# RWKV-7 group of a hybrid decoder: the token mean taken from the turned values, the state's products accumulated in PSUM, the square taken by ScalarE

## The reference, cut to what matters

```
def step(S, inp):                      # for each of the 512 tokens
    r_t, w_t, k_t, v_t, kk_t, a_t = inp
    sa = einsum('bhvk,bhk->bhv', S, -kk_t)
    S = S * w_t[:, :, None, :] + sa[..., None] * (kk_t * a_t)[:, :, None, :] + v_t[..., None] * k_t[:, :, None, :]
    return S, einsum('bhvk,bhk->bhv', S, r_t)
...
y = _wkv7_scan(r, decay, k, v, kk, a)
y = _group_norm(y, ln_w, ln_b, RW_GN_EPS) + sum(r * k * r_k, -1) * v
```

## Time and profile before

| | |
|---|---|
| device time, median of 3 runs | 2413.65 us (2412.28 to 2413.82) |
| the profiled execution's own time | 2416.05 us |
| its span, first to last instruction | 2414.3 us |
| granted TensorE clock, mean over the span | 0.99 |
| TensorE busy (matmul) | 2324.0 us, 96% of the span |
| GpSimd busy | 1737.8 us, 72% |
| VectorE busy | 1192.2 us, 49% |
| ScalarE busy | 634.9 us, 26% |

### The profile page before, as it was taken

The page is one execution under the profiler, slowest core; times in us unless marked ns, Lnnn a source line. Parts: engine busy times, 40 slices in busy tenths (PEclk is TensorE's granted clock), DMA queues, the critical chain, the costliest instruction groups (busy, mean ns, idle before and its releaser), DMA issues. The chain is left out here.

```text
span 2414.3 us, 38594 instructions
## 1 busy us (share of the span) xinstructions
PE 2324.0 (96%) x16160; PEld 1751.9 (73%) x16160; DVE 1192.2 (49%) x1515; ACT 634.9 (26%) x1133; POOL 1737.8 (72%) x1228
## 2 busy tenths in 40 slices
PE   7999999999999999899999999999999999989999
PEld 6767777777777777677777677777776777767777
DVE  5123346647464773565250323557375546735552
ACT  5222222212221222333341323222222212214421
POOL 3677688768577787687637666878586687877785
PEclk9999999999999999999999999999999999999999
DMA  4623253223234346432445233533242243473323
GB/s 156 187 80 104 83 161 110 84 81 114 84 89 132 118 131 233 151 92 71 148 112 160 79 114 92 154 93 102 66 121 82 81 150 108 131 275 110 86 77 125
DMA packets 164335, 285.09 MB, mean 118 GB/s; under 512 B 28664, under 2 KB 36216, under 8 KB 162624
## 3 DMA queue, kind: packets, MB, share of 16 engines
q1 hardware_dynamic: 108352, 180.93, 27.0%
q10 hardware_dynamic: 55808, 101.69, 12.4%
HBM read 230.89 MB, written 51.64 MB: 117 GB/s over the span
## 5 line engine op out<-in xcount | busy, mean ns | idle before, releaser
L733 POOL TENSOR_SCALAR w_hi<-raw 128x512 fp32r<-128x512 f32 x552 | 905.4, 1640 | 476.3 <-PE ps_proj L774 401.6
L743 POOL TENSOR_TENSOR w_lo<-raw,w_hi 128x512 fp32r<-128x512 f32 (+1 forms) x640 | 836.8, 1308 | 152.6 <-ACT w_hi L1237 97.1
L774 PE MATMUL ps_proj<-h_hi,w_hi 128*128 128x512 f32 (+1 forms) x1760 | 740.1, 421 | 2.0 <-POOL w_lo L743 0.9
L774 PE MATMUL ps_proj<-h_lo,w_hi 128*128 128x512 f32 (+1 forms) x1760 | 691.8, 393 | 0.0
L774 PE MATMUL ps_proj<-h_hi,w_lo 128*128 128x512 f32 x1728 | 678.5, 393 | 0.0
L774 PEld LDWEIGHTS ps_proj<-h_hi,w_hi 128*128 128x128 f32 (+1 forms) x1760 | 331.3, 188 | 113.1 <-issue 29.7
L774 PEld LDWEIGHTS ps_proj<-h_lo,w_hi 128*128 128x128 f32 (+1 forms) x1760 | 331.3, 188 | 75.0
L774 PEld LDWEIGHTS ps_proj<-h_hi,w_lo 128*128 128x128 f32 x1728 | 327.8, 190 | 68.6 <-issue 11.4
L789 PE MATMUL ps_proj<-w_hi,h_hi 128*128 128x512 f32 x448 | 181.1, 404 | 0.4 <-POOL w_lo L743 0.4
L789 PE MATMUL ps_proj<-w_hi,h_lo 128*128 128x512 f32 x448 | 174.9, 390 | 0.0
L789 PE MATMUL ps_proj<-w_lo,h_hi 128*128 128x512 f32 x448 | 174.5, 390 | 0.0
(11 more groups left out here) (349 smaller groups left out, 3132.5 us busy)
## 6 DMA issues: line engine op xcount, KB each, us to landing
raw<-in_w_in_dram SPq DMA_DIRECT2D x480, 256.0 KB, 2.7
raw<-in_w_out_dram SPq DMA_DIRECT2D x128, 256.0 KB, 3.0
projected<-stage ACTq DMA_DIRECT2D x116, 256.0 KB, 2.8
arena<-projected ACTq DMA_DIRECT2D x90, 256.0 KB, 3.1
out_dram<-arena ACTq DMA_DIRECT2D x7, 1024.0 KB, 4.8
gated_hi<-arena ACTq DMA_DIRECT2D x24, 256.0 KB, 2.6
gated_lo<-arena ACTq DMA_DIRECT2D x24, 256.0 KB, 3.2
h_hi<-gated_hi SPq DMA_DIRECT2D x8, 768.0 KB, 13.7
```

The source lines that it names most:

```text
L733: nc.gpsimd.tensor_scalar(hi, src, 1.0, None, ALU.mult).then_inc(s_hi_split, 1)
L743: nc.gpsimd.tensor_tensor(lo, src, hi.bitcast(F32), ALU.subtract).then_inc(s_raw_split, 1)
L774: last = mm(ps_proj[rows, m, :], lhsT, rhs, start=(k == 0 and j == 0), stop=(k == KT - 1 and j == len(products) - 1))
```

## The change

The mean is no longer taken from the output but from the values, when they lie turned in PSUM: VectorE sums each token's 64 elements (`tensor_reduce` to a new `rw_vmean`) and writes `rw_vT = v - sum / 64`, in place of ScalarE's copy. TensorE's mean product and its waits go. The state's products are added onto the local output in banks 2 and 3, for the chunks 1 to 7 alone (the state ahead of chunk 0 is zero), so VectorE's copy of the local output, its zero state and its two additions go. ScalarE squares the output in PSUM, VectorE multiplies it there by one over the root. The local products are issued in another order: all of the first kind, then those of the output, in which only the first tile's products carry `start`. Of the fills, `rw_v` goes from 2 to 4 tiles, `rw_carried` from 2 to 3, and `rw_mean` (3 tiles) goes.

```diff
-    rw_turned=(3, 3, 3, 3), rw_v=(2, 2, 2, 2),
+    rw_turned=(3, 3, 3, 3), rw_v=(4, 4, 4, 4),
-    rw_carried=(2, 2, 2, 2), rw_mean=(3, 3, 3, 3), rw_gate=(13, 14, 13, 12),
+    rw_carried=(3, 3, 3, 3), rw_gate=(13, 14, 13, 12),
+        y_parts = ps[:, 2:4, 256:512].rearrange("p c (i t) -> p c i t", i=NT)
...  TensorE
                         fill("rw_v", hp)
+                        pe.wait_ge(s_rw_turned_copied, 3 * hp + 3)
                         pe.wait_ge(s_rw_v_copied, hp + 1)
...
                             for c, q, h, half in quarters:
                                 mm(ps[half, 2 + c, own], rw_pu[...], rw_gb[...], start=True, stop=True)
+                        for i in range(NT):
+                            fed = slice(256 + i * 64, 256 + (i + 1) * 64)
                             for c, q, h, half in quarters:
-                                mm(ps[half, 2 + c, fed], rw_vT[...], rw_gk[...], start=True, stop=False)
+                                mm(ps[half, 2 + c, fed], rw_vT[...], rw_gk[...], start=(i == 0), stop=False)
                             for c, q, h, half in quarters:
-                                mm(ps[half, 2 + c, fed], rw_pu[...], rw_gb[...], start=False, stop=True)
+                                mm(ps[half, 2 + c, fed], rw_pu[...], rw_gb[...], start=False, stop=False)
...
-                        for c in range(NCH):
+                        for c in range(1, NCH):
+                            fed = slice(256 + c // 2 * 64, 256 + c // 2 * 64 + 64)
                             for h in range(2):
-                                last = mm(ps[half, 2 + h, c * 64:(c + 1) * 64], rw_st[half, c, :], rw_ar[...],
-                                          start=True, stop=True)
+                                last = mm(ps[half, 2 + c % 2, fed], rw_st[half, c, :], rw_ar[...],
+                                          start=False, stop=(c >= NCH - 2))
                         last.then_inc(s_rw_carried, 1)
                         fill("rw_carried", hp)
-                        pe.wait_ge(s_rw_y_whole, hp + 1)
-                        mm(ps[:, 0, :], bones, rw_yl, start=True, stop=True).then_inc(s_rw_mean, 1)
-                        fill("rw_mean", hp)
-                        pe.wait_ge(s_rw_centred, hp + 1)
+                        pe.wait_ge(s_rw_y_squared, hp + 1)
                         mm(ps[:, 1, :], bones, rw_sq, start=True, stop=True).then_inc(s_rw_var, 1)
...  ScalarE
-                        act.wait_ge(s_rw_v_turned, hp + 1)
-                        nc.scalar.activation(rw_vT, ps[:, 0, :]..., ACT.Copy).then_inc(s_rw_v_copied, 1)
...
+                        act.wait_ge(s_rw_carried, hp + 1)
+                        nc.scalar.activation(rw_sq.rearrange(...), y_parts, ACT.Square).then_inc(s_rw_y_squared, 1)
                         fill("rw_carried", hp)
...  VectorE, behind the bonus term (L1852)
+                        dve.wait_ge(s_rw_v_turned, hp + 1)
+                        v_turned = ps[:, 0, :].rearrange("p (i h c) -> p i h c", i=NT, h=2)
+                        link(v.tensor_reduce(rw_vmean, v_turned, AX, ADD))
+                        v.scalar_tensor_tensor(out=rw_vT..., in0=rw_vmean[:, :, :, None].to_broadcast([P, NT, 2, 64]),
+                                               scalar=-1.0 / 64, in1=v_turned, op0=MUL, op1=ADD).then_inc(s_rw_v_copied, 1)
...  VectorE, local output and state
-                        link(v.tensor_copy(rw_yl..., ps[:, 2:4, 256:512]...))
                         link(v.tensor_tensor(rw_wli, eye64..., last_w, MUL))
...
-                        v.memset(rw_st[:, 0, :], 0.0).then_inc(s_rw_local_ready, 1)
...  VectorE, behind the carry
-                        (the two additions of L1902, L1909 and L1910, with their waits)
                         dve.wait_ge(s_rw_rstd, hp + 1)
-                        link(v.tensor_tensor(rw_yl, rw_yl, rw_nr, MUL))
+                        link(v.tensor_tensor(rw_yl..., rw_nr..., y_parts, MUL))
```

More of the change, by code:

```diff
@@ L98 @@
     la_probs=(13, 13, 13, 13), la_turned=(3, 3, 3, 3), la_gate=(4, 4, 4, 4),
-    rw_first=8, rw_lora=(10, 10, 10, 9), rw_factors=(31, 33, 33, 33), rw_turned=(3, 3, 3, 3), rw_v=(2, 2, 2, 2),
+    rw_first=8, rw_lora=(10, 10, 10, 9), rw_factors=(31, 33, 33, 33), rw_turned=(3, 3, 3, 3), rw_v=(4, 4, 4, 4),
     rw_gram=(4, 4, 4, 4), rw_x=(2, 2, 2, 2), rw_level=(1, 1, 1, 1), rw_step=(1, 1, 1, 1), rw_levels=(1, 1, 1, 1),
     rw_pu=(2, 2, 2, 2), rw_local=(4, 4, 4, 4), rw_outer=(1, 1, 1, 1), rw_state=(1, 1, 1, 1), rw_state_last=(0, 0, 0, 0),
-    rw_carried=(2, 2, 2, 2), rw_mean=(3, 3, 3, 3), rw_gate=(13, 14, 13, 12),
+    rw_carried=(3, 3, 3, 3), rw_gate=(13, 14, 13, 12),
     ml_first=25, ml_qk=(19, 10, 10, 10), ml_s=(8, 7, 7, 6), ml_h=(14, 14, 13, 11), ml_gate=(7, 12, 12, 12),
@@ L275, in planned @@
             place("rw_state", h, j)
-        for name in ("rw_state_last", "rw_carried", "rw_mean"):
+        for name in ("rw_state_last", "rw_carried"):
             place(name, h)
@@ L428, in build @@
         rw_wl = rg(NCH)
+        rw_vmean = rg(NT, 2)
         ml_early = rg.at
@@ L592, in build @@
         s_rw_carried = sem("rw_carried")
-        s_rw_y_whole = sem("rw_y_whole")
-        s_rw_mean = sem("rw_mean")
-        s_rw_centred = sem("rw_centred")
+        s_rw_y_squared = sem("rw_y_squared")
         s_rw_var = sem("rw_var")
@@ L1065, in _ @@
                         for i in range(NT):
-                            own, fed = slice(i * 64, (i + 1) * 64), slice(256 + i * 64, 256 + (i + 1) * 64)
+                            own = slice(i * 64, (i + 1) * 64)
                             for c, q, h, half in quarters:
@@ L1069, in _ @@
                                    start=True, stop=True)
+                        for i in range(NT):
+                            fed = slice(256 + i * 64, 256 + (i + 1) * 64)
                             for c, q, h, half in quarters:
                                 mm(ps[half, 2 + c, fed], rw_vT[q, i, half], rw_gk[q, 4 * h + i, 64:P],
-                                   start=True, stop=False)
+                                   start=(i == 0), stop=False)
                             for c, q, h, half in quarters:
                                 mm(ps[half, 2 + c, fed], rw_pu[q, 4 * h + i, 64:P], rw_gb[q, 4 * h + i, 64:P],
-                                   start=False, stop=True)
+                                   start=False, stop=False)
                         fill("rw_outer", hp)
@@ L1100, in _ @@
                         pe.wait_ge(s_rw_state_ready, (NCH - 2) * (hp + 1))
-                        for c in range(NCH):
+                        for c in range(1, NCH):
+                            fed = slice(256 + c // 2 * 64, 256 + c // 2 * 64 + 64)
                             for h in range(2):
                                 half = slice(64 * h, 64 * h + 64)
-                                last = mm(ps[half, 2 + h, c * 64:(c + 1) * 64], rw_st[half, c, :],
+                                last = mm(ps[half, 2 + c % 2, fed], rw_st[half, c, :],
                                           rw_ar[half, c // 2, 1, 64 * (c % 2):64 * (c % 2) + 64],
-                                          start=True, stop=True)
+                                          start=False, stop=(c >= NCH - 2))
                         last.then_inc(s_rw_carried, 1)
                         fill("rw_carried", hp)
-                        pe.wait_ge(s_rw_y_whole, hp + 1)
-                        mm(ps[:, 0, :], bones, rw_yl, start=True, stop=True).then_inc(s_rw_mean, 1)
-                        fill("rw_mean", hp)
-                        pe.wait_ge(s_rw_centred, hp + 1)
+                        pe.wait_ge(s_rw_y_squared, hp + 1)
                         mm(ps[:, 1, :], bones, rw_sq, start=True, stop=True).then_inc(s_rw_var, 1)
@@ L1476, in _ @@
                         fill("rw_turned", hp)
-                        act.wait_ge(s_rw_v_turned, hp + 1)
-                        nc.scalar.activation(rw_vT, ps[:, 0, :].rearrange("p (i c) -> p i c", i=NT), ACT.Copy).then_inc(s_rw_v_copied, 1)
                         fill("rw_v", hp)
@@ L1510, in _ @@
                         fill("rw_state_last", hp)
+                        act.wait_ge(s_rw_carried, hp + 1)
+                        nc.scalar.activation(rw_sq.rearrange("p (i c t) -> p c i t", i=NT, c=2), y_parts, ACT.Square).then_inc(s_rw_y_squared, 1)
                         fill("rw_carried", hp)
-                        fill("rw_mean", hp)
                         act.wait_ge(s_rw_var, hp + 1)
@@ L1852, in _ @@
                         v.tensor_tensor(rw_bonus, ps[:, 3, :], vv, MUL).then_inc(s_rw_bonus_ready, 1)
+                        dve.wait_ge(s_rw_v_turned, hp + 1)
+                        v_turned = ps[:, 0, :].rearrange("p (i h c) -> p i h c", i=NT, h=2)
+                        link(v.tensor_reduce(rw_vmean, v_turned, AX, ADD))
```

(12 more changed lines are left out.)

1 line of the change is left out of this document (removed).

## The result

The changed kernel takes 2391.86 us in the median of four runs (2388.64 to 2396.16), the one before 2413.74 beside it: a ratio of 0.9902, 95% interval 0.9888 to 0.9915; the medians lie 21.9 us apart. Its profiled execution took 2396.16 us, against 2416.05 before: 19.9 us between the two that the traces describe. The forecast was 2395.

What follows compares the result with a forecast made beforehand. TensorE's in-order stream, 96% covered by matmuls, was taken as the bound. Terms 8.4 + 3.3 + 1.1 + 3.7 + 2.0 = 18.5 us, off the median 2413.65, gave 2395; range 2390 to 2402.

Steps and rivals of the forecast that it cites:

- the gate chain: VectorE's scaling through L1817: 1.0 us less at L963 in each of two fourth passes, 2.0 in all; bounds 0 and 3.9.
- the masks: VectorE's L1863 and L1864, for the ladder's first products: taken as 0, bounds minus 3.4 and plus 2.4 us.
- The mean product: TensorE's L1110 goes from all eight passes: 8.4 us less.
- The wait at the variance: TensorE's wait at L1113 for VectorE's square L1910 goes, as ScalarE squares instead: 3.3 us less over eight passes.
- The state's products: Chunk 0's two of 16 calls at L1104 go, adding in PSUM costs nothing: 1.1 us less over eight passes.
- The start of the carry: VectorE's copy L1883 and memset go ahead of the first L1095: 0.47 us less a pass, 3.7 in all.
- The turned values: VectorE's sum and write before L985 take about 1.5 us under 2.77 us of fill: no cost, 1.2 us spare.
- The rival of values that come late: VectorE's sum or write before L985 is slow: 7 us, 2402; chance 0.04 still faster, 0.02 slower.
- ScalarE's tables: One more ScalarE table load, 1.28 us, for the logarithm after the square, stays hidden: no cost.
- its rival for the worse: VectorE's lock moves: the 2.0 us at L963 fail, L1864 costs 2.4 more; 14.1 us gain, 2399.5; chance 0.14.
- the one for the better: VectorE's lock falls better at L963 and L1864, 1.9 + 3.4 us more: 2390; chance 0.06.
- GpSimd as the bound: GpSimd's splits in long fills before L967 take back 0.9 us in each of four passes, 3.6: 2399; chance 0.10.

## Why the prediction was right, point by point

**The sum.** The forecast was 18.5 us less. The medians gave 21.9, by the interval of the ratio 20.5 to 27.0; so the time lies inside the stated range, but the sum fell short by at least 2 us. The first four terms came as forecast, 16.4 by the traces against 16.5. What the sum lacks lies in the gate chain, the turning of the factors and the masks.

**The bound.** TensorE's stream sets the time, and a float32 product in a fill costs what it pushes back: shown by the product put back alone, 0.86 us a piece in the trace.

**The mean product** (forecast 8.4): left whole, 8.4. Of it 6.9 are the product and 1.5 its wait and start.

**The wait at the variance** (3.3): 3.4. That VectorE's instruction was to blame, and not a fill too short, is shown by the square on ScalarE alone. That it was for its operands in SBUF is shown for the scaling, not for the square; the square's rows only fit it.

**The state's products** (1.1): 0.9, from 1.28 to 1.17 us a pass. Adding in PSUM costs nothing that the trace shows (32 records in 1.15 us before, 28 in 1.03 after), and the local products in their new order cost 1.76 us a pass, as before.

**The start of the carry** (3.7): 3.7, and 3.6 in the kernel before by order alone.

**The turned values** (nothing, with 1.2 us to spare): both new instructions took 0.69 us in all passes, and they ended 1.24 us before the Gram products began. That they were to be covered by more than two tiles is shown by the run with two. The rival of values that come late needed 5.1 us; it was off by 3.7.

**ScalarE's tables** (hidden): the load ran from 447.82 to 449.10, the variance was issued at 449.25 and finished about a microsecond later. The load began 0.02 us after the square, and the trace shows nothing of the drain that the Trainium skill, "ScalarE: Activation LUTs", section "What ACT_TABLE_LOAD costs", adds to it. Nor does one stand behind a load: in the kernel before, ScalarE's next instruction began at 453.96, 0.02 us after the load of the earlier trace rows.

**The gate chain** (2.0): this is the term that was sized too small. L963 fell by 4.4 us, of which 0.3 is the first pass that the change doesn't reach. The two fourth passes gave 3.4 and the other four 0.7, which the sum had at nothing. I had counted 0.98 us of shorter product against a wait of 1.70. But VectorE's next instructions fell on other moments of GpSimd's cycle too, some better, some worse, so the chain to L1817 got shorter by more than the one instruction: from the start of the scaling to the end of L1817 it took 15.0 us before and 12.9 after in the chains that end in the third and fourth passes. It ended at 656.98 in the fourth pass, 0.61 us ahead of TensorE, where before it was 1.44 late. So all of L963's waiting behind the first pass went, the upper bound of the prediction; it had this at 3.9, by the same reading it is 4.1. The run with the scaling from SBUF shows that it hangs on this one operand. That the other instructions would fall well was luck: the forecast had no way to know it, and its rival for the worse had a chance of 0.14, the one for the better 0.06.

**The turning of the factors** (nothing): 0.8 less. It waits further on in VectorE's same stream, for L1850, and went back to 18.9 us with the scaling from SBUF. The prediction ended the chain at L1817.

**The masks** (0, from -3.4 to +2.4): -1.0; in the three runs with other fills +0.7, -0.2 and, where they have a tile more to hide under, -2.8 against the kernel before. The sign was not to be had from the profile of before; the size stayed inside the bounds.

**GpSimd as the bound.** It did not become it. One sign of being wrong did appear: the wait of projection products for GpSimd, which was not to grow above 0.9 us, is 1.4 in the changed kernel's profile and 0.9 in its second one, half a microsecond at the most. The lead, from the end of a split to its first use, was used up at another place than I had it. I had said that TensorE gets 2.1 us ahead per pass against a lead of 1.2. The rows of the changed kernel's timeline, fourth pass of the second layer, where the lead was 2.6 us before:

```profile
1866.05 1.46 POOL L743 TENSOR_TENSOR w_lo<-raw,w_hi 128x512 fp32r<-128x512 f32 x1
...
1867.75 0.39 PE L774 MATMUL ps_proj<-h_hi,w_hi 128*128 128x512 f32 x1
```

That is 0.24 us. In the second passes, where L963 had next to no wait to lose, the lead is 1.4 us (1.2 before); in the third and fourth 0.56 and 0.53 in the first layer, 0.30 and 0.24 in the second. With the mean product back (0.86 us more a pass, ahead of the long fill) they are the same to 0.06 us; with L963's waits back they are 1.2 and 2.6 again. So what TensorE wins ahead of the long fills moves GpSimd too, as the prediction said, and the lead falls where TensorE wins inside them. It falls by more than that: by 0.6 and 0.9 us in the third passes and 2.0 and 2.4 in the fourth, where L963 gave 0.3 and 1.7. No run shows where the rest comes from. That the next 0.3 us won inside would be GpSimd's to give is argued from the leads; no run took more there.

## What to carry to other kernels

Where TensorE's stream is full, price an edit by what it pushes back there, place by place: products that go are won nearly in full, and work taken off another engine is won only where a wait names it, though it can move other waits of the same chain. A wait that is long in some passes and short in others, for the same instructions, can come from a collision: compare minimum and maximum of the instruction before lengthening its cover, and give it an operand in PSUM, or another engine. And before a second such gain, look at how much lead the engine that feeds the stream has inside that stretch, not on the average.

## What the runs showed of the hardware that was not expected

VectorE's instructions with one tensor in SBUF as their input are held beside GpSimd as well, not only those with two. In the changed kernel, minimum, median and maximum in ns of L1816, a product of a tensor and a scalar for each partition, and of L1847, a copy of eight columns:

```profile
L1816 DVE TENSOR_SCALAR arena<-arena,par x8: 577/1074/1400, 370.1 to 1842.7; 128x512 f32<-128x512 f32 x8
...
L1847 DVE COPY arena<-arena x8: 324/394/1149, 391.2 to 1866.4; 128x8 f32<-128x8 f32 x8
```

The longest of these copies began 0.34 us after the subtraction of 1866.05 that is shown above, and ended 0.03 us behind it:

```profile
1866.39 1.15 DVE L1847 COPY arena<-arena 128x8 f32<-128x8 f32 x1
```

It goes the other way too: GpSimd's L733, 1.49 us when nothing is in its way, took 2.39 us where it began (658.69) while VectorE's scan L1822, which has two inputs in SBUF, was running (657.63 to 659.80), and 1.93 at 1864.04, where L1843 ran until 1864.61. Not every overlap costs: L1845 began at 1865.67, 0.30 us before that L733 ended, and took 0.69 us. All VectorE instructions of 128x512 with an operand in PSUM that were looked at (L1852, L1855, L1856, L1908) took 0.686 to 0.693 us every time. The subtraction L743 took up to 1.66 us in the stretch of the earlier trace rows (at 490.36), not 1.46, but the ones that the long squares ran into took 1.30: there only VectorE, which began later, stood.
